# GDN and GLA heads on one Trainium2 core: a Sqrt of a constant ahead of the squares, and four pieces of work moved

## The chip, the cores and the metric

The program runs on one core of a Trainium2 chip. The time is device microseconds of one execution. Five engines work side by side and meet at semaphores: PE (matrix products), ACT (activations), DVE (vector work), POOL (vector work; here all its operands lie in SBUF), SP (here it only issues transfers). PE reads SBUF and writes PSUM.

## The reference

A four-layer trunk in one streaming step: 512 tokens of a new stream and 16 tokens of each of 8 running streams. Order of the parts: FFN, GLA mixer, FFN, FFN, gated-delta (GDN) mixer, FFN, each closed by a layer norm. The change lies in the two mixers. Of GDN, per value head and chunk:

```python
m = jnp.where(strict, jnp.einsum('bhid,bhjd->bhij', kb, kc) * decay, 0.0)
sol = lax.linalg.triangular_solve(eye + m, rhs, ...)     # w, u
v_new = u - jnp.einsum('bhid,bhdv->bhiv', w, s)
o = q_decayed @ s + att @ v_new
s = jnp.exp(g_last) * s + jnp.einsum('bhjd,bhjv->bhdv', k_end, v_new)
...
o = rms_norm(o, norm_g) * jax.nn.silu(z)                 # then @ w_o
```

q and k pass a short convolution, a silu and an l2 norm ahead of it. GLA has a recurrence of the same kind without the solve, and the same rms norm and silu gate.

## The kernel before

All 640 tokens stay in SBUF. Weights come in chunks of 128 columns, alternately into two buffers (`raw[0]`, `raw[1]`). ACT casts a chunk to `wh` (`act_split`, L246), POOL subtracts to get the rest `wl` (L283), and PE multiplies with both parts (L559 in the mixers, L228 in FFNs and projections). A chunk's buffer `wh` may be written again only when its tile of products is done.

Every engine runs its own program in the order in which it is written; nothing reorders. On PE the tile products of the *next* head are cut into 48 parts (`parts(a, b)`) that stand between the small products of the present head, so that PE has work while ACT and DVE prepare the next small product. GDN has 8 heads in two halves; after heads 3 and 7 stands an output projection. Head 7 has no next head: only parts 32 to 47 stand in it.

The steps of a GDN head that the change touches, in order:

- Start: PE transposes q and k (L544). ACT takes ten squares with a running sum (L1386), DVE adds epsilon (L1557), ACT takes the root (L1389), DVE inverts and scales (L1559, L1561, L1564, L1565). PE waits for that ahead of the transposes of v (L544 again).
- Later the four conv tiles of the next head come out of PSUM (`tile_out(0..3)`: three copies and a cast), and their silu (`conv_end`).
- Sequential part, t = 0 to 3: PE L1239, L1240, L1258, L1266, L1270; ACT `new_values` (L1443), `from_state` (L1437), `squares` (L1428); DVE `less_old` (L1665), the state (L1716), `outputs` (L1672). Then the running streams as a fifth step: PE L1275, L1281, L1292; DVE decays the eight streams' states in two halves (L1678), spreads values (L1684), adds outputs.
- Turn: DVE L1728, ACT root (L1461), DVE `new_stream(0)` (L1692), inverse (L1731), scaling of the outputs (L1734), `new_stream(1)`. PE transposes the outputs (L1300) when L1734 and both `new_stream` are done. ACT: silu of z (L1378) and cast of two tiles (`tile_out(4)`, `tile_out(5)`). DVE gates (L1698) and splits (L961, L963). PE goes on with the first part of the next head's conv tile (L559), which needs the `wl` of the chunk that `tile_out(4)` cast.

ACT holds one set of function tables at a time. A load (ACT_TABLE_LOAD) is put into ACT's program ahead of the first function that needs another set. Square and Copy need none of their own here; Sqrt, Exp and Silu do. In GLA the same pattern stands at a head's end: five squares (L849), DVE L937, root (L852).

Of the kernel before, what the change touches and what calls it, by code (L numbers as in the profile page):

```python
# [108 lines left out]
def build(nc, wstream, x_in, consts, ln_cols, w_a1, w_a2, b_a, norm_cols, w_ab, a_dt, conv_w, hist_in,  # L109
          gla_s, gdn_s, y_out, gla_p_out, gdn_p_out, hist_out, gla_s_out, gdn_s_out):  # L110
    with ExitStack() as ctx:
# [126 lines left out]
        def act_split(act, T, par):  # L238

            if isinstance(T, int) and T + 2 >= N_CHUNKS:  # L240
                return
            nxt = half(T) + 1
            act.wait_ge(loaded[par].sem, loaded[par].at(nxt))
            if not (isinstance(T, int) and T < 0):
                act.wait_ge(tile_done.sem, tile_done.at(T))
            act.copy(wh[:, par, :], raw[:, par, :]).then_inc(hi_ready.sem, hi_ready.by)  # L246
# [529 lines left out]
        def gla_loop(eng, body):  # L776
            with eng.Fori(0, GLA_HEADS - 1) as i:
                body(i)
            body(GLA_HEADS - 1, last=True)

        def act_gla(act, occ):
            b = base["gla", 0]

            def copy_in(T, par, j):
                act.wait_ge(tile_done.sem, tile_done.at(T))
                act.copy(halves(a_in[j]), slot(par)).then_inc(evacuated[par].sem, evacuated[par].by)
                act_split(act, T, par)
            copy_in(b, 0, 0)
            act.wait_ge(gla["rank_mm"].sem, gla["rank_mm"].at(0))
            act.copy(halves(a_rank), msc[:, 0:2, 0:HALF])\  # L790
               .then_inc(gla["rank"].sem, gla["rank"].by)
            copy_in(b + 1, 1, 1)
            for t in range(TT):
                ab = a_abs[:, t % 2, :]
                act.wait_ge(gla["logit_mm"].sem, gla["logit_mm"].at(0, t))
                if t >= 2:
                    act.wait_ge(gla["la"].sem, gla["la"].at(0, t - 2))
                act.activation(ab, msc[:, 2 + t % 2, :], ACT.Abs).then_inc(gla["logit_act"].sem, gla["logit_act"].by)
                act.wait_ge(gla["logit_act"].sem, gla["logit_act"].at(0, 3 * t))
                act.activation(ab, ab, ACT.Exp, scale=-1.0).then_inc(gla["logit_act"].sem, gla["logit_act"].by)  # L800
                act.wait_ge(gla["logit_act"].sem, gla["logit_act"].at(0, 3 * t + 1))
                act.activation(ab, ab, ACT.Ln, bias=ones[:, 0:1]).then_inc(gla["logit_act"].sem, gla["logit_act"].by)
            copy_in(b + 2, 0, 2)
            copy_in(b + 3, 1, 3)

            def body(i, last=False):
                h = i

                def tile_out(n):

                    j, par = GLA_ORDER[n], n % 2
                    if last and j < 4:
                        return
                    T = gla_tile(i, j)
                    act.wait_ge(tile_done.sem, tile_done.at(T))
                    if j >= 4:
                        act.activation(halves(a_z[j - 4]), slot(par), ACT.Silu).then_inc(evacuated[par].sem, evacuated[par].by)
                    else:

                        act.copy(halves(a_in[j]), slot(par)).then_inc(evacuated[par].sem, evacuated[par].by)  # L820
                    act_split(act, T, par)
                act.dma_start(a_sin.rearrange("p s d n -> p s (d n)"), gla_s[h]).then_inc(a_sld.sem, a_sld.by)
                act.wait_ge(gla["v_mm"].sem, gla["v_mm"].at(h, 0))
                act.copy(a_vt[:, :, 0:P], tiles5(pair[1])).then_inc(gla["v"].sem, gla["v"].by)
                act.wait_ge(gla["v_mm"].sem, gla["v_mm"].at(h, 1))
                act.copy(a_vt[:, :, P:2 * P], tiles5(pair[0])).then_inc(gla["v"].sem, gla["v"].by)
                act.wait_ge(gla["bs"].sem, gla["bs"].at(h))
                act.activation(a_e, a_bs, ACT.Exp, scale=1.0 / GATE_TAU).then_inc(gla["exp"].sem, gla["exp"].by)
                act.activation(a_en, a_bs, ACT.Exp, scale=-1.0 / GATE_TAU).then_inc(gla["exp"].sem, gla["exp"].by)
                act.wait_ge(gla["kdiff"].sem, gla["kdiff"].at(h))  # L830
                act.activation(a_kd, a_kd, ACT.Exp, scale=1.0 / GATE_TAU).then_inc(gla["kexp"].sem, gla["kexp"].by)
                tile_out(0)
                act.wait_ge(gla["ke_mm"].sem, gla["ke_mm"].at(h))
                act.copy(a_ket, tiles5(pair[0])).then_inc(gla["ke"].sem, gla["ke"].by)
                tile_out(1)
                for n in range(NCK):
                    if n % 2:
                        act.wait_ge(gla["o_mm"].sem, gla["o_mm"].at(h, n))
                        act.copy(a_o[:, n // 2, :], msc[:, (n // 2) % 2, 0:2 * P]).then_inc(gla["o"].sem, gla["o"].by)
                    if n in (2, 5):  # L840
                        tile_out(2 if n == 2 else 3)
                tile_out(4)
                act.wait_ge(gla["mid"].sem, gla["mid"].at(h))
                act.copy(a_o[:, PT, :], msc[:, 0, 0:2 * P]).then_inc(gla["o"].sem, gla["o"].by)
                for t in range(TT):
                    act.wait_ge(gla["o"].sem, gla["o"].at(h, t))
                    if t:
                        act.wait_ge(gla["sq"].sem, h * TT + t)
                    ins = act.activation(a_sq, a_o[:, t, :], ACT.Square, accum_out=a_ss[:, t:t + 1])  # L849
                    ins.then_inc(gla["sq"].sem, 1)  # L850
                act.wait_ge(gla["ss"].sem, gla["ss"].at(h))
                act.activation(a_std, a_ss, ACT.Sqrt).then_inc(gla["std"].sem, gla["std"].by)  # L852
                tile_out(5)

                act.wait_ge(gla["s_new"].sem, gla["s_new"].at(h, 1))
                act.dma_start(gla_s_out[h], a_sin.rearrange("p s d n -> p s (d n)")).then_inc(a_sst.sem, a_sst.by)
                act.dma_start(gla_p_out[h], a_s).then_inc(a_sst.sem, a_sst.by)
                act.wait_ge(a_sst.sem, a_sst.at(h, 1))
            gla_loop(act, body)
            act_projection(act, ("gla", 0), b + GLA_HEADS * 6, stats=True)  # L860

# [451 lines left out]
        def act_gdn(act, occ):  # L1313
# [46 lines left out]
            def body(hf, i, last=False):  # L1360
# [5 lines left out]
                        freed = (gdn["qk_mm"], s, j) if j < 2 else (gdn["v_mm"], s, j - 2)  # L1366
                        conv_out(j, s * 4 + (4 + j), freed)

                def tile_out(j):

                    T = gdn_tile(hf, i, j, last)
                    if j < 4:
                        if not last:
                            conv_in(T, j % 2, s * 4 + (4 + j), False)
                        return
                    act.wait_ge(tile_done.sem, tile_done.at(T))
                    act.wait_ge(gdn["att"].sem, gdn["att"].at(s, 1))
                    act.activation(halves(d_z[j - 4]), slot(j % 2), ACT.Silu).then_inc(evacuated[j % 2].sem, evacuated[j % 2].by)  # L1378
                    act_split(act, T, j % 2)
                for j in range(2):  # L1380
                    act.wait_ge(gdn["qk_mm"].sem, gdn["qk_mm"].at(s, j))
                    for t in range(TT):
# [35 lines left out]
                act.wait_ge(gdn["y_mm"].sem, gdn["y_mm"].at(s, product(LEVELS - 1, 1)))  # L1418
                act.dma_start(d_sin, gdn_s[s]).then_inc(d_sld.sem, d_sld.by)
                tile_out(3)  # L1420

                def squares(t):
                    for v in range(2):
# [21 lines left out]
                for t in range(PT):  # L1445
                    if t == 0:
                        new_values(t)
                        act.wait_ge(gdn["att"].sem, gdn["att"].at(s, 1))
                        from_state(t)
                    else:  # L1450
                        from_state(t)
                        new_values(t)
                        squares(t - 1)
                    if t == 3:
                        conv_end(3)
                from_state(PT)
                new_values(PT)
                squares(3)
                squares(4)
                act.wait_ge(gdn["oss"].sem, gdn["oss"].at(s))  # L1460
                act.activation(d_ors, d_os, ACT.Sqrt).then_inc(gdn["ostd"].sem, gdn["ostd"].by)  # L1461
                tile_out(4)
                tile_out(5)
                act.wait_ge(gdn["s_new"].sem, gdn["s_new"].at(s, 1))
                act.dma_start(gdn_s_out[s], d_sin).then_inc(d_sst.sem, d_sst.by)
                act.dma_start(gdn_p_out[s], d_s).then_inc(d_sst.sem, d_sst.by)
            for hf in range(2):
                gdn_in_line(hf, body)
                act_projection(act, ("gdn", 0), proj_start(hf), stats=hf == 1)

        def dve_gdn(dve, occ):
# [74 lines left out]
            def body(hf, i, last=False):  # L1546
# [154 lines left out]
                for t in range(PT):  # L1701
# [5 lines left out]
                        convolve(3, range(2 * t - 2, 2 * t))  # L1707
                    if t == 3:
                        less_old(PT)
                    dve.wait_ge(gdn["su_mm"].sem, gdn["su_mm"].at(s, t))  # L1710
                    if t == 0:
                        dve.wait_ge(gdn["s_zero"].sem, gdn["s_zero"].at(s))
# [6 lines left out]
                    ins.then_inc(gdn["state"].sem, gdn["state"].by)  # L1719
                    outputs(t)  # L1720
                key_ends(PT)
                decay_stream(0)
                decay_stream(1)
                dve.wait_ge(gdn["vn"].sem, gdn["vn"].at(s, PT))
                spread_values()
# [200 lines left out]
```

## Time and profile before

| | us |
|---|---|
| median of 3 runs (lowest, highest) | 3195.5 (3193.84, 3204.11) |
| profiled execution, own time | 3201.72 |
| its span, first to last instruction | 3199.8 |
| PE busy | 3043.3 (95%) |
| DVE, ACT, POOL busy | 1328.1, 1013.1, 994.8 |

GLA lies between about 505 and 840 us of the span, GDN between about 1830 and 2690. In a timeline row the first number is the start, the second the time taken, the bracket at its end the engine's idle time before it and what ended that. Busy time of PE does not tell at which clock it ran; the granted clock is a column of the stretches view.

### The profile page before, as it was taken

Reading aid. Unit: us, or ns where it says so; the run is one execution under the profiler, and the core shown is the slowest. Engines: PE = TensorE matmul, PEld = TensorE weight load, DVE = VectorE, ACT = ScalarE, POOL = GpSimd, SP = SyncE. Lnnn points to the kernel's source line nnn. Section 1 sums busy time; section 2 is a strip of 40 time slices with the busy share of each in tenths; the row PEclk is TensorE's granted clock in tenths of the full one; section 3 lists DMA queues with packets and bytes.
Section 4 is the critical chain, followed back from the end, with each engine's and each line's share of the span. In section 5 each row is a group of like instructions: output and inputs, shape, how many; then the busy total and the mean of one; then the engine's idle time right before and its main releaser. Section 6 shows DMA issues by size and latency. Waiting matters only on the chain.

```text
span 3199.8 us, 61556 instructions
## 1 busy us (share of the span) xinstructions
PE 3043.3 (95%) x25790; PEld 2904.8 (91%) x25790; DVE 1328.1 (42%) x1923; ACT 1013.1 (32%) x1751; POOL 994.8 (31%) x412
## 2 busy tenths in 40 slices
PE   8999999998999999999999989999999889999997
PEld 8999997887899999899999878888988778999997
DVE  3212253335521313621312666676376655312226
ACT  2111126333341111432111445444354434321112
POOL 3333343221433333433333411111211104333332
PEclk9999999999999999999999989999999979999998
DMA  3222221222122222122222111111111111222222
GB/s 132 73 77 80 74 82 51 81 75 83 60 73 74 79 79 77 64 74 77 73 86 73 63 45 62 62 69 63 67 62 69 63 43 53 79 73 79 80 73 78
DMA packets 62317, 230.60 MB, mean 72 GB/s; under 512 B 8257, under 2 KB 10177, under 8 KB 58754
## 3 DMA queue, kind: packets, MB, share of 16 engines
q1 hardware_dynamic: 56898, 200.27, 17.8%
q10 hardware_dynamic: 5184, 26.74, 2.2%
q8 instruction: 203, 3.33, 0.4%
q14 instruction: 32, 0.26, 0.0%
HBM read 209.76 MB, written 17.22 MB: 71 GB/s over the span
## 4 chain that ended last, share of the span: by engine, by line
PE 70%; issue 21%; POOL 4%; DVE 4%; ACT 1%; POOLq 0%; DVEq 0%; ACTq 0%
PE gem L228 60%; PE gem L559 4%; POOL wl L283 3%; POOL xl L509 1%; PE msc L420 1%; PE msc L435 1%; PE msc L726 1%; PE msc L734 1%; PE msc L544 0%; DVE work L497 0%; DVE work L925 0%; DVE work L928 0%; ACT small L1386 0%; PE msc L722 0%; DVE hh L961 0%
## 5 line engine op out<-in xcount | busy, mean ns | idle before, releaser
L283 POOL TENSOR_TENSOR wl<-raw,wh 128x1024 fp32r<-128x1024 f32 x368 | 931.9, 2533 | 2117.2 <-ACT wh L246 2117.2
L246 ACT CAST wh<-raw 128x1024 fp32r<-128x1024 f32 x368 | 386.5, 1050 | 1426.3 <-PE gem L228 1403.9
L228 PE MATMUL gem<-xh,wh 128*128 128x320 f32 x2688 | 612.6, 309 | 5.0 <-POOL wl L283 5.0
L228 PE MATMUL gem<-xl,wh 128*128 128x320 f32 x2688 | 612.5, 309 | 0.0
L228 PE MATMUL gem<-xh,wl 128*128 128x320 f32 x2688 | 612.4, 309 | 0.0
L228 PEld LDWEIGHTS gem<-xh,wh 128*128 128x128 f32 x2688 | 449.3, 188 | 5.9 <-ACT work L329 5.4
L228 PEld LDWEIGHTS gem<-xh,wl 128*128 128x128 f32 x2688 | 449.5, 188 | 0.0
L228 PEld LDWEIGHTS gem<-xl,wh 128*128 128x128 f32 x2688 | 449.3, 188 | 0.0
L350 DVE TENSOR_TENSOR work<-work,gem 128x640 f32<-128x640 f32 x88 | 72.3, 821 | 879.4 <-PE gem L228 843.4
L228 PE MATMUL gem<-hh,wh 128*128 128x320 f32 x1792 | 409.1, 310 | 2.1 <-issue 2.1
L228 PE MATMUL gem<-hl,wh 128*128 128x320 f32 x1792 | 408.9, 309 | 0.0
L228 PE MATMUL gem<-hh,wl 128*128 128x320 f32 x1792 | 408.8, 309 | 0.0
L559 PE MATMUL gem<-xh,wh 128*128 128x320 f32 x1184 | 302.6, 337 | 9.1 <-POOL wl L283 6.5
L228 PEld LDWEIGHTS gem<-hh,wh 128*128 128x128 f32 x1792 | 300.2, 188 | 2.5 <-issue 2.5
L228 PEld LDWEIGHTS gem<-hh,wl 128*128 128x128 f32 x1792 | 300.2, 188 | 0.0
L228 PEld LDWEIGHTS gem<-hl,wh 128*128 128x128 f32 x1792 | 300.0, 188 | 0.0
L378 DVE SCALAR_TENSOR_TENSOR x<-x,gem 128x640 f32 (+1 forms) x120 | 98.6, 822 | 482.1 <-PE gem L228 482.1
L559 PE MATMUL gem<-xl,wh 128*128 128x320 f32 x1184 | 274.4, 313 | 8.0 <-POOL xl L509 7.9
L559 PE MATMUL gem<-xh,wl 128*128 128x320 f32 x1184 | 272.3, 311 | 0.7 <-issue 0.6
L355 DVE TENSOR_TENSOR hl<-work,hh 128x640 f32 (+1 forms) x88 | 242.6, 2757 | 10.7
L559 PEld LDWEIGHTS gem<-xh,wh 128*128 128x128 f32 x1184 | 193.2, 192 | 35.9 <-issue 29.1
L559 PEld LDWEIGHTS gem<-xl,wh 128*128 128x128 f32 x1184 | 199.7, 190 | 13.2 <-POOL xl L509 13.2
(266 smaller groups left out, 2924.3 us busy)
## 6 DMA issues: line engine op xcount, KB each, us to landing
raw<-wstream SPq DMA_DIRECT2D x368, 512.0 KB, 3.5
work<-gdn_s ACTq DMA_DIRECT2D x8, 1024.0 KB, 5.0
gdn_s_out<-work ACTq DMA_DIRECT2D x8, 1024.0 KB, 4.0
work<-gla_s ACTq DMA_DIRECT2D x4, 1024.0 KB, 6.9
gla_s_out<-work ACTq DMA_DIRECT2D x4, 1024.0 KB, 4.0
x<-x_in SPq DMA_DIRECT2D x2, 1280.0 KB, 8.1
y_out<-x SPq DMA_DIRECT2D x8, 320.0 KB, 2.2
gdn_p_out<-work ACTq DMA_DIRECT2D x8, 128.0 KB, 4.0
```

What stands on the lines that cost most here:

```text
L228: mm = pe.matmul(gem[:, par, s, 0:HALF], w, r[:, k, s * HALF:(s + 1) * HALF], start=(k == 0 and n == 0), stop=(k == kts - 1 and n == 2))
L246: act.copy(wh[:, par, :], raw[:, par, :]).then_inc(hi_ready.sem, hi_ready.by)
L283: pool.tensor_tensor(wl[:, par, :], raw[:, par, :], wh[:, par, :].bitcast(F32), ALU.subtract)\
L350: dve.tensor_tensor(halves(hid), halves(gate), slot(1), ALU.mult)\
L355: dve.tensor_tensor(hl[:, i, :], hid, hh[:, i, :].bitcast(F32), ALU.subtract)\
L378: dve.scalar_tensor_tensor(out=halves(xt), in0=halves(xt), scalar=scale, in1=slot(par), op0=ALU.mult, op1=ALU.add).then_inc(evacuated[par] ...
L420: mm = pe.matmul(msc[:, 0, a * 8 + t:a * 8 + t + 1], src[:, t * P:(t + 1) * P], cs[:, C_MEAN:C_MEAN + 1], start=first and a == t == 0, sto ...
L435: pe.matmul(msc[:, b + s, 0:HALF], ones, flat[:, s * HALF:(s + 1) * HALF], start=True, stop=True)\
L509: pool.tensor_tensor(xl[:, k, :], x[:, k, :], xh[:, k, :].bitcast(F32), ALU.subtract)\
L559: mm = pe.matmul(gem[:, par, s, 0:HALF], w, r[:, k, s * HALF:(s + 1) * HALF], start=(k == 0 and n == 0), stop=(k == KT - 1 and n == 2))
L726: pe.matmul(msc[:, 2 + c, 0:2 * P], a_ket[rows, t, :], a_vt[rows, t, :], start=True, stop=True)\
L734: pe.matmul(msc[rows, t % 2, 0:2 * P], a_qd[:, n * GLA_CHUNK:(n + 1) * GLA_CHUNK], a_s, start=False, stop=True, skip_group_check=True)\
```

## The change

A new helper, `root_table`, takes the Sqrt of one constant column (128x1) into an unused column of `small`. It is called at three places: in GLA behind `tile_out(1)`, in a GDN head at its start, and in a GDN head behind `tile_out(3)`, ahead of the sequential part. The number of table loads in the program stays at 75. In the turn, the cast of `tile_out(4)` goes ahead of its silu; `conv_end(3)` goes from t = 3 to behind the two stores of the states; DVE's first half of the decay goes from behind the fifth step's `key_ends` to t = 3, ahead of the state update.

```diff
+        def root_table(act):
+            act.activation(small[:, 56:57], ones[:, 0:1], ACT.Sqrt)
...
                 tile_out(1)
+                root_table(act)
                 for n in range(NCK):
...
-                def tile_out(j):
+                def tile_out(j, split_done=False):
...
                     act.activation(halves(d_z[j - 4]), slot(j % 2), ACT.Silu).then_inc(...)
-                    act_split(act, T, j % 2)
+                    if not split_done:
+                        act_split(act, T, j % 2)
+                root_table(act)
                 for j in range(2):
                     act.wait_ge(gdn["qk_mm"].sem, gdn["qk_mm"].at(s, j))
...
                 tile_out(3)
+                root_table(act)
...
                         squares(t - 1)
-                    if t == 3:
-                        conv_end(3)
                 from_state(PT)
...
                 act.activation(d_ors, d_os, ACT.Sqrt).then_inc(gdn["ostd"].sem, gdn["ostd"].by)
-                tile_out(4)
+                act_split(act, gdn_tile(hf, i, 4, last), 0)
+                tile_out(4, split_done=True)
                 tile_out(5)
                 act.wait_ge(gdn["s_new"].sem, gdn["s_new"].at(s, 1))
                 act.dma_start(gdn_s_out[s], d_sin).then_inc(d_sst.sem, d_sst.by)
                 act.dma_start(gdn_p_out[s], d_s).then_inc(d_sst.sem, d_sst.by)
+                conv_end(3)
...
                     if t == 3:
                         less_old(PT)
+                        decay_stream(0)
...
                 key_ends(PT)
-                decay_stream(0)
                 decay_stream(1)
```

On ACT at the turn of a GDN head, from `conv_end(3)` (L1332) to the first cast (L246), before:

```order
L1332 ACTIVATE work<-work 128x512
L1333 ACTIVATE work<-work 128x128
L1437 ACTIVATE work<-msc,gq 128x128 x2
L1443 ACTIVATE work<-msc,gq 128x128 x2
L1428 ACTIVATE small,gq<-work 128x128 x4
L1461 ACT_TABLE_LOAD
L1461 ACTIVATE gq<-gq 128x10
L1378 ACT_TABLE_LOAD
L1378 ACTIVATE work<-gem 128x640
L246 CAST wh<-raw 128x1024
```

And of the changed kernel, from `new_values` of the fifth step (now L1451) to the load for the new Sqrt (L783) that opens the next head:

```order
L1451 ACTIVATE work<-msc,gq 128x128 x2
L1436 ACTIVATE small,gq<-work 128x128 x4
L1467 ACTIVATE gq<-gq 128x10
L246 CAST wh<-raw 128x1024
L1383 ACT_TABLE_LOAD
L1383 ACTIVATE work<-gem 128x640 x2
L246 CAST wh<-raw 128x1024
L1472 DMA gdn_s_out<-work 128x2048
L1473 DMA gdn_p_out<-work 128x256
L1337 ACTIVATE work<-work 128x512
L1338 ACTIVATE work<-work 128x128
L783 ACT_TABLE_LOAD
```

The load stands no longer between the last squares and the root, the first cast follows the root at once, and the silu of the conv tile stands behind the two stores.

On ACT ahead of the sequential part, from the load of the streams' states (DMA) on, before:

```order
L1419 DMA work<-gdn_s 128x2048
L1321 COPY work<-gem 128x320
L1322 COPY work<-gem 128x192
L1323 COPY work<-gem 128x8x16
L246 CAST wh<-raw 128x1024
L1443 ACTIVATE work<-msc,gq 128x128 x2
```

And of the changed kernel:

```order
L1426 DMA work<-gdn_s 128x2048
L1326 COPY work<-gem 128x320
L1327 COPY work<-gem 128x192
L1328 COPY work<-gem 128x8x16
L246 CAST wh<-raw 128x1024
L783 ACT_TABLE_LOAD
L783 ACTIVATE small<-cs 128x1
L1451 ACTIVATE work<-msc,gq 128x128 x2
```

A load and the new Sqrt stand between the cast of the fourth conv tile and `new_values` of t = 0.

On DVE at t = 3 and behind it (`less_old`, state, outputs, `key_ends`, decay, spread), before:

```order
L1665 SCALAR_TENSOR_TENSOR work<-msc,gq,work 128x128 x4
L1716 SCALAR_TENSOR_TENSOR work<-work,gq,msc 128x128 x2
L1672 TENSOR_TENSOR work<-work,msc 128x256
L1656 TENSOR_SCALAR work<-work,gq 128x128 x2
L1678 TENSOR_TENSOR work<-work,gq 128x1024 x2
L1684 TENSOR_SCALAR work<-work,cs 128x2x128 x2
```

And of the changed kernel:

```order
L1673 SCALAR_TENSOR_TENSOR work<-msc,gq,work 128x128 x4
L1686 TENSOR_TENSOR work<-work,gq 128x1024
L1725 SCALAR_TENSOR_TENSOR work<-work,gq,msc 128x128 x2
L1680 TENSOR_TENSOR work<-work,msc 128x256
L1664 TENSOR_SCALAR work<-work,gq 128x128 x2
L1686 TENSOR_TENSOR work<-work,gq 128x1024
L1692 TENSOR_SCALAR work<-work,cs 128x2x128 x2
```

One of the two decays now stands ahead of the state update. PE's, POOL's and SP's programs keep their order.

## Rows read from the trace of the kernel before

**Rows 1.** The chain that ended last, by engine, from the page

```profile
PE 70%; issue 21%; POOL 4%; DVE 4%; ACT 1%; POOLq 0%; DVEq 0%; ACTq 0%
```

**Rows 2.** Who PE waited for, GDN stretch: us in total, times, longest

```profile
PE msc L544 <- DVE work L1564: 8.3, 7, 6.3
...
PE msc L1275 <- ACT work L1437: 6.3, 7, 1.1
...
PE gem L559 <- POOL wl L283: 5.5, 5, 1.1
```

**Rows 3.** Timeline of PE, one turn (head 1 to head 2)

```profile
2043.68 0.71 PE L1275 MATMUL msc<-work 128*128 128x128 f32 x4 [0.85 <-ACT work L1437]
...
2047.59 1.15 PE L1292 MATMUL msc<-work 32*128 32x256 f32 x16 [0.89 <-DVE work L1672]
...
2052.94 1.28 PE L1300 MATMUL msc<-cs,work 128*128 128x128 f32 x10 [0.50 <-DVE work L1692]
...
2055.33 0.53 PE L559 MATMUL gem<-xh,wh 128*128 128x320 f32 x2 [1.11 <-POOL wl L283]
```

**Rows 4.** Timeline of ACT, the same turn and the squares behind it

```profile
2042.31 0.61 ACT L1332 ACTIVATE work<-work 128x512 f32<-128x512 f32 x1
...
2048.28 1.28 ACT L1461 ACT_TABLE_LOAD   x1
2049.57 0.21 ACT L1461 ACTIVATE gq<-gq 128x10 f32<-128x10 f32 x1
...
2051.70 1.04 ACT L246 CAST wh<-raw 128x1024 fp32r<-128x1024 f32 x1
...
2057.03 0.28 ACT L1386 ACTIVATE small<-msc 128x128 f32<-128x128 f32 x1 [2.75 <-PE msc L544]
...
2061.07 1.28 ACT L1389 ACT_TABLE_LOAD   x1
```

**Rows 5.** Timeline of DVE, the same turn

```profile
2042.87 0.61 DVE L1716 SCALAR_TENSOR_TENSOR work<-work,gq,msc 128x128 f32<-128x128 f32 x2 [2.16 <-PE msc L1270]
...
2044.11 2.36 DVE L1678 TENSOR_TENSOR work<-work,gq 128x1024 f32<-128x1024 f32 x2
...
2048.29 0.17 DVE L1728 TENSOR_SCALAR gq<-gq 128x10 f32<-128x10 f32 x1 [0.96 <-ACT small L1428]
2048.79 1.22 DVE L1692 TENSOR_TENSOR work<-work,msc 128x1024 f32<-128x1024 f32 x1 [0.33 <-PE msc L1292]
...
2050.17 1.49 DVE L1734 TENSOR_TENSOR work<-work,gq 128x1280 f32<-128x1280 f32 x1
```

**Rows 6.** Timeline of POOL, the same turn

```profile
2052.81 4.71 POOL L283 TENSOR_TENSOR wl<-raw,wh 128x1024 fp32r<-128x1024 f32 x2 [28.39 <-ACT wh L246]
```

**Rows 7.** Timeline of ACT at the start of a sequential part, head 2

```profile
2110.15 1.07 ACT L246 CAST wh<-raw 128x1024 fp32r<-128x1024 f32 x1
2111.74 0.62 ACT L1443 ACTIVATE work<-msc,gq 128x128 f32<-128x128 f32 x2 [0.52 <-PE msc L1258]
```

**Rows 8.** Timeline of DVE at the start of a sequential part, head 2

```profile
2110.86 0.82 DVE L1600 TENSOR_TENSOR work<-work 128x640 f32<-128x640 f32 x1
```

**Rows 9.** Timeline of DVE, the same place in head 1

```profile
2022.26 2.84 DVE L1600 TENSOR_TENSOR work<-work 128x640 f32<-128x640 f32 x1
```

**Rows 10.** Timeline of POOL, the same place in head 1

```profile
2022.04 2.38 POOL L283 TENSOR_TENSOR wl<-raw,wh 128x1024 fp32r<-128x1024 f32 x1 [20.07 <-ACT wh L246]
```

**Rows 11.** Busy time by stretch; behind POOL's: granted PE clock, DMA share, GB/s

```profile
2004.00:2021.00 17.00, 15.81 (x220) 13.96 (x206) 8.93 (x25) 5.40 (x18) 0.00 (x0) 0.61 0.14 44
...
2547.00:2551.00 4.00, 1.53 (x10) 1.06 (x10) 3.96 (x4) 2.79 (x16) 2.94 (x2) 0.93 0.91 328
2051.50:2056.50 5.00, 3.40 (x25) 2.95 (x24) 4.08 (x5) 2.78 (x4) 3.69 (x2) 1.00 0.56 225
```

**Rows 12.** Timeline of ACT at a GLA head's end

```profile
604.35 0.21 ACT L852 ACTIVATE small<-small 128x5 f32<-128x5 f32 x1 [3.03 <-DVE small L937]
```

**Rows 13.** Timeline of ACT behind `tile_out(1)` in the last GLA head

```profile
761.89 0.37 ACT L839 COPY work<-msc 128x256 f32<-128x256 f32 x1 [1.27 <-PE msc L734]
```

## The prediction

> **What bounds the kernel now.** I first read the chain that ended last: 70% of it is PE [rows 1]. An edit on ACT, DVE or POOL therefore counts only where PE waits for it. Then I read who PE waits for in the GDN stretch, and the timelines of PE, ACT, DVE and POOL round one turn. In 2040 to 2060 us PE stands still four times: 0.85 us ahead of L1275 (for ACT's `from_state`), 0.89 ahead of L1292 (for DVE's last `outputs`), 0.50 ahead of L1300 (for `new_stream(1)`), 1.11 ahead of the next head's L559 (for POOL's `wl`) [rows 3]. A fifth wait, ahead of the transposes of v, is for the scaling behind the first root: 8.3 us in 7 waits, 6.3 of it in one (head 7, which has no tile products to fill it), so 0.33 in each other [rows 2]. Together 3.7 us per turn. The reader is to see that these waits are links of one sequence: a gain in one moves the start of the next.
>
> **Part 1, fifth step.** `conv_end(3)` leaves the stretch between the squares of t = 2 and `from_state`. Its first silu begins at 2042.31 [rows 4], and PE waits 0.85 for what stands behind it [rows 3]; 6.3 us in 7 heads [rows 2]. `from_state` can start about 0.6 us earlier (0.61 and the tail of a shorter one; they overlap the next instruction). One decay goes to t = 3, where DVE stands idle for 2.16 us ahead of the state update [rows 5]. One decay is half of 2.36, or 1.18 us [rows 5], so that idle time covers it; were it gone, the state and all behind it would be up to 1.18 later. Behind the state only one decay is left, and spread and outputs follow 1.14 earlier (the other decay now ends about when the new values are there). L1292 starts 1.14 earlier: 0.6 of it from ACT, the rest out of the 0.89.
>
> **Part 2, the root of the turn.** The load of 1.28 us at 2048.28 goes [rows 4]. But DVE, between its L1728 and L1734, has `new_stream(0)` to do, which waits for L1292 and ends near 2050.0; the root with its load is done at 2049.78 [rows 4, 5]. So the load lay beside work, and removing it alone gives 0.
>
> **Part 3, the cast goes ahead.** In the old times: L1728 ends at 2048.46, the root of 0.21 at about 2048.7, the cast (1.04) at about 2049.7, and POOL starts some 0.07 behind a cast, as it does at 2052.81 behind the cast that ends at 2052.74 [rows 4 to 6]. So POOL starts near 2049.8 rather than at 2052.81, and the wait of 1.11 for `wl` goes. What is late next? POOL's instruction takes 2.36 (half of 4.71 [rows 6]), so it runs to about 2052.1, and L1734 becomes ready at 2050.17 [rows 5], inside it. In head 1, DVE's L1600, ready at 2022.26, met a POOL instruction of 2022.04 to 2024.42: it ended at 2025.10, 2.84 long, where the same line takes 0.82 in head 2 [rows 8 to 10]. It ended 0.68 behind POOL's end, so 0.14 of its 0.82 had been done in the wait. L1734, like L1600, reads two operands from SBUF and writes SBUF. If it waits in the same way, it ends 1.49 - 0.14 = 1.35 behind POOL's end: 2052.11 + 1.35 = 2053.46, in place of 2051.66, or 1.80 later. `new_stream(1)` and L1300 are 1.80 later with it. Bounds of this term: 0, if L1734 gets in ahead of POOL or doesn't mind it, and 2.0, if the small inverse ahead of L1734 waits too. I take 1.80: POOL is ready about 0.4 us ahead of L1734, more than the error of these sums.
>
> On this the Trainium skill (GPSIMD Engine Reference, 8. Key points) says that GpSimd shares its SBUF interfaces with VectorE and contends with DVE instructions in a 2-port perf mode or with two SBUF inputs. By that rule L1734 is one that collides, and L1692 and L1698, which read PSUM, are not; the trace agrees as far as L1600 goes, and shows no L1734 under a POOL instruction.
>
> So L1300 starts 1.80 - 1.14 = 0.66 later than before, at 2053.6, and PE waits there 2.3 us, not 0.50. It ends at about 2054.9, `wl` is long there, and L559 starts 0.4 earlier than at 2055.33.
>
> **Part 4, the next head's start.** ACT now issues two stores and then does the silu of `conv_end(3)` (0.9), a load (1.28) and the new Sqrt (0.2) ahead of the squares. ACT stood idle for 2.75 us there [rows 4]; with the stores waiting for the later `new_stream(1)` it is ready about when the transposes are, some 0.3 earlier than at 2057.03. Behind the squares the load at 2061.07 is gone [rows 4]; the root still waits for L1557, so 1.05 to 1.1 us is left as gain, and the wait of 0.33 ahead of the transposes of v goes. Turn in all: 0.40 + 0.33, or 0.73 earlier.
>
> **Part 5, ahead of the sequential part.** Here the new load is on the path. The cast ends at 2111.22 and `new_values` starts at 2111.74, as soon as PE's L1258 lets it [rows 7]. With 1.28 and 0.21 in between it starts near 2112.7: 0.93 later. PE does one part meanwhile and is at L1266 when the new values come; the rest of the step goes through them. So 0.93 in each of heads 0 to 6. Head 7 has no fourth tile there and pays 0. Bounds: 0.5 to 1.0.
>
> The Trainium skill (ScalarE: Activation LUTs, What ACT_TABLE_LOAD costs) gives about 1283 ns for the load and 1380 more for a drain. The load is confirmed; the Sqrt behind the load starts at 2049.57, 0.01 after it, so no drain of that length is seen. By the page this part would cost 2.3 us a head, an estimate.
>
> **Part 6, GLA.** The root there waits for DVE (3.03 idle [rows 12]) and the load lies in that; removing it gives 0. Its new place has 1.27 idle in the tightest head [rows 13], against 1.49: 0.2 late in a copy that PE needs over 1 us later. 0 in all.
>
> **The sum.** Turns 0-1, 1-2, 2-3, 4-5 and 5-6: 5 x 0.73 = 3.7 gained. Turns into the two projections: 0.4 and 0.3 gained (no gain behind them: head 4's squares now start behind ACT's load, which takes what the missing one gives). Turn 6-7: 0.15 lost (L1300 later, no tile product to regain it). Together 4.2 gained. Heads 0 to 6: 7 x 0.93 = 6.5 lost. Net 2.3 us slower. The profiled execution would go from 3201.72 to 3204.0. It stands 6.2 above the median; head 1 in it lost about 17 x 0.39 = 6.6 us to the clock at 0.61 in one 17 us stretch [rows 11], which need not fall in every run. From the median of 3195.5 I forecast 3198.
>
> **Rivals.** First, L1734 gets in ahead of POOL, or they don't collide there. Then L1300 starts 1.14 earlier, the `wl` wait of 1.11 goes as well, and behind the squares 0.2 more (there ACT's own silu and load are the bound): 2.45 a turn, 5 x 2.45 + 2.25 + 2.25 + 0.9 = 17.7, less 6.5: 3184. For it: only 0.4 us of lead. Against it: POOL's start hangs on one short root and one cast of known length, L1734 on PE's L1292 and 1.22 of DVE. 17%.
>
> Second, slower: the longer waits bring the granted clock to its lower level. Over 2547 to 2551 us, where PE was busy 1.53 of 4.00 with transposes alone, the clock fell to 0.93 of that stretch and on; in 2051.5 to 2056.5, busy 3.40 of 5.00, it stayed at 1.00 [rows 11]. By the main case the turn holds 2.3 us of rest and 1.28 of transposes in one piece. The price of one fall, from the stretch in head 1, is up to 6.6 us: one gives 3204, two 3211. It decides from two falls on. 18%.
>
> Third, a load holds ACT for longer than its own row, say twice its 1.28 [rows 4], at the place where PE waits for it. Seven times 1.28 is 9.0 more: 3207. The drain of the Trainium skill's page above would be such a hold. The root that starts 0.01 behind its load [rows 4] speaks against it. 3%.
>
> That nothing changes at all (the loads keep their number, 75) falls into the main case's range.
>
> **How the numbers follow.** Main case 62%, its own range 3192 to 3203. Rival one 17%, two 18%, three 3%. The range is to hold the time 8 times in 10: 3185 to 3208, cutting off half of the first rival and the worse part of the second. A measurement of this kernel tells 0.3%, or 9.6 us, from no change (its three runs lie 10 us apart). Faster by that is the first rival alone, and not quite all of it: 0.16. Slower: two falls or more, or the drain, 0.18. The rest, 0.66, is no change.
>
> **What would show it.** In the changed profile: L1275's wait down to about 0.2 and L1292's to about 0.4; decay at t = 3 inside DVE's idle time; the L1734 line (then L1742) near 3.2 us long, not 1.49, under POOL's instruction; PE's wait ahead of L1300 (then L1305) near 2.3; none for `wl` behind it; a new wait of about 0.9 ahead of L1266 (then L1271) in seven heads. The forecast is wrong if L1742 is 1.49 long (then it is faster), or if PE doesn't wait at L1271.

## The result, and the profile after

Over 20 runs each the changed kernel takes 3205.76 us in the median (3199.74 to 3213.59), the kernel before 3196.73 (3192.27 to 3205.71). The ratio is 1.0024, 95% interval 1.0017 to 1.0031: 7.7 us slower (5.4 to 9.9), below the 0.3% that the prediction set as a bound, and inside its range. Forecast were 2.3 us more. The profiled execution takes 3201.40 us, 4 below its median; that of before stood 5 above its own.

What PE waits for in the GDN stretch (answers to [rows 2]; total, times, longest):

```profile
PE msc L1305 <- DVE work L1700: 18.5, 8, 2.4
...
PE msc L544 <- DVE work L1572: 5.6, 2, 5.3
PE msc L1271 <- ACT work L1451: 5.0, 7, 0.7
...
PE msc L1297 <- DVE work L1680: 3.7, 8, 0.5
...
PE msc L544 <- ACT work L1400: 2.6, 6, 0.5
```

The wait for `wl` (5.5) is gone, `from_state` and `outputs` (6.3 and 7.5) have shrunk to about 1.1 and 3.7. In their place: 18.5 ahead of the turn's transposes (L1305, before 4.0) and 5.0 ahead of L1271, which PE waited for once before.

The turn from head 1 to head 2, on PE (answers to [rows 3]):

```profile
2035.38 0.71 PE L1280 MATMUL msc<-work 128*128 128x128 f32 x4
...
2038.86 1.15 PE L1297 MATMUL msc<-work 32*128 32x256 f32 x16 [0.46 <-DVE work L1680]
...
2046.13 1.93 PE L1305 MATMUL msc<-cs,work 128*128 128x128 f32 x10 [2.41 <-DVE work L1700]
```

The same on ACT (to [rows 4]), DVE (to [rows 5]) and POOL (to [rows 6]):

```profile
2039.87 0.21 ACT L1467 ACTIVATE gq<-gq 128x10 f32<-128x10 f32 x1 [0.24 <-DVE gq L1736]
2039.99 1.03 ACT L246 CAST wh<-raw 128x1024 fp32r<-128x1024 f32 x1
```

```profile
2033.03 1.21 DVE L1686 TENSOR_TENSOR work<-work,gq 128x1024 f32<-128x1024 f32 x1
2035.28 0.61 DVE L1725 SCALAR_TENSOR_TENSOR work<-work,gq,msc 128x128 f32<-128x128 f32 x2 [1.03 <-PE msc L1275]
...
2041.44 3.41 DVE L1742 TENSOR_TENSOR work<-work,gq 128x1280 f32<-128x1280 f32 x1
```

```profile
2041.10 2.40 POOL L283 TENSOR_TENSOR wl<-raw,wh 128x1024 fp32r<-128x1024 f32 x1 [22.89 <-ACT wh L246]
```

This is the main case of the prediction: POOL starts 0.34 us ahead of the scaling, the scaling takes 3.41 us and not 1.49, and PE rests 2.41. The first decay lies inside idle time of DVE.

The start of a sequential part, on ACT (answers to [rows 7]) and PE:

```profile
2014.47 1.07 ACT L246 CAST wh<-raw 128x1024 fp32r<-128x1024 f32 x1
2015.56 1.28 ACT L783 ACT_TABLE_LOAD   x1
2016.85 0.20 ACT L783 ACTIVATE small<-cs 128x1 f32<-128x1 f32 x1
2016.96 0.61 ACT L1451 ACTIVATE work<-msc,gq 128x128 f32<-128x128 f32 x2
```

```profile
2015.34 0.69 PE L1263 MATMUL msc<-work 128*128 128x128 f32 x4
2017.62 0.71 PE L1271 MATMUL msc<-work 128*128 128x128 f32 x4 [0.72 <-ACT work L1451]
```

The same two products on PE before, head 2:

```profile
2111.02 0.69 PE L1258 MATMUL msc<-work 128*128 128x128 f32 x4
...
2112.43 0.70 PE L1266 MATMUL msc<-work 128*128 128x128 f32 x4
```

From start to start it was 1.41 us and is 2.28, so the new load costs 0.87 a head, 6.1 in seven heads. The bracket says only 0.72: it counts from the end of the product before, and without a wait L1266 starts 0.16 ahead of that end.

What was not in the main case stands in the stretches view: two turns, 0-1 and 1-2 (us, busy time of PE, PEld, DVE, ACT, POOL; behind POOL's the granted clock; answers to the last line of [rows 11]).

```profile
1956.80:1962.60 5.80, 3.50 (x30) 3.22 (x29) 4.84 (x6) 3.82 (x6) 2.39 (x2) 1.00 0.72 271
2043.40:2050.40 7.00, 4.59 (x26) 4.32 (x25) 5.74 (x7) 3.96 (x6) 2.46 (x2) 0.76 0.74 259
```

Both have nearly the same rest (2.30 and 2.41). In the second the clock fell to its lower level: the ten transposes take 1.93 us there and 1.28 in the first (next rows, PE, then ACT's first square), and the squares start 4.35 behind them and not 3.20. Up to the squares, one fall costs the turn 1.15 us.

```profile
1959.44 1.28 PE L1305 MATMUL msc<-cs,work 128*128 128x128 f32 x10 [2.30 <-DVE work L1700]
```

```profile
1962.64 0.26 ACT L1393 ACTIVATE small<-msc 128x128 f32<-128x128 f32 x1
...
2050.48 0.28 ACT L1393 ACTIVATE small<-msc 128x128 f32<-128x128 f32 x1 [1.08 <-PE msc L544]
```

Further on it is more. The turn from L1275 of t = 3 to the first L1151 of the next head, turn 0-1 and then 1-2:

```profile
1948.04 0.61 PE L1275 MATMUL msc<-work 128*128 128x128 f32 x4
...
1974.27 2.39 PE L1151 MATMUL msc<-work 128*128 128x128 f32 x20
```

```profile
2034.63 0.61 PE L1275 MATMUL msc<-work 128*128 128x128 f32 x4
...
2062.54 2.39 PE L1151 MATMUL msc<-work 128*128 128x128 f32 x20
```

And turn 1-2 before:

```profile
2042.22 0.61 PE L1270 MATMUL msc<-work 128*128 128x128 f32 x4
...
2069.10 2.39 PE L1146 MATMUL msc<-work 128*128 128x128 f32 x20
```

That is 26.23 us without a fall, 27.91 with one, and 26.88 before. So a fall costs 1.6 to 1.7 (turn 2-3 takes 27.83), and a turn without one is 0.65 shorter than before.

Four of the eight turns of this execution fall at the wait; before, all eight stayed up. What decides it isn't shown: the shortest rest (2.24, turn 2-3) is among those that fall, and three turns with 2.30 don't. That the two profiled executions are equally long comes from another fall: that of before has the loss of up to 6.6 us in head 1 [rows 11], this one has not.

### The profile page after: what moved, and what is told of

Same layout as the page of the kernel before. It is cut to its first block, busy times and chain, and to the rows that moved or that the text cites. A ratio compares the mean times of both kernels' runs of the same rounds, so it can differ in the third digit from the quotient of the medians.

```text
span 3199.5 us, 61576 instructions
## 1 busy us (share of the span) xinstructions
PE 3043.8 (95%) x25790; PEld 2908.1 (91%) x25790; DVE 1324.2 (41%) x1923; ACT 1017.6 (32%) x1771; POOL 995.8 (31%) x412
## 4 chain that ended last, share of the span: by engine, by line
PE 81%; DVE 8%; issue 5%; ACT 3%; POOL 2%; DVEq 0%; ACTq 0%; POOLq 0%
PE gem L228 62%; PE gem L559 9%; POOL xl L509 2%; PE msc L420 1%; DVE work L1500 1%; PE msc L435 1%; PE msc L544 1%; PE msc L1184 1%; DVE work L1597 1%; PE msc L1176 1%; PE msc L726 1%; PE msc L734 1%; PE msc L1271 1%; POOL wl L283 1%; PE msc L1151 0%
## 5 line engine op out<-in xcount | busy, mean ns | idle before, releaser
L246 ACT CAST wh<-raw 128x1024 fp32r<-128x1024 f32 x368 | 386.3, 1050 | 1425.1 <-PE gem L228 1403.6
L559 PE MATMUL gem<-xh,wh 128*128 128x320 f32 x1184 | 301.8, 336 | 4.0 <-issue 1.6
L559 PE MATMUL gem<-xl,wh 128*128 128x320 f32 x1184 | 274.0, 313 | 6.6 <-POOL xl L509 6.5
L559 PE MATMUL gem<-xh,wl 128*128 128x320 f32 x1184 | 272.0, 311 | 0.4 <-issue 0.3
L559 PEld LDWEIGHTS gem<-xh,wh 128*128 128x128 f32 x1184 | 192.9, 191 | 28.8 <-issue 22.1
L559 PEld LDWEIGHTS gem<-xl,wh 128*128 128x128 f32 x1184 | 199.4, 190 | 11.0 <-POOL xl L509 10.8
```

Of the source, the lines that this page charges most:

```text
L559: mm = pe.matmul(gem[:, par, s, 0:HALF], w, r[:, k, s * HALF:(s + 1) * HALF], start=(k == 0 and n == 0), stop=(k == KT - 1 and n == 2))
```

## The experiments

The theory after this reading: the excess is the collision at the turn, plus the falls in the rest that it makes, plus the seven waits ahead of L1271 (5.0 us by their brackets). Each kernel was timed against the kernel before on the same chip; differences are the ratio less one, times 3196.

| kernel | against before, us (95%) |
|---|---|
| changed kernel | +7.7 (5.4 to 9.9) |
| e1: no Sqrt ahead of the sequential part | -18.9 (-24 to -13) |
| e2: cast behind its silu | -11.8 (-17 to -7) |
| e3: neither | -11.8 (-17 to -7) |
| e4: 16 products in the rest | +9.6 (5.4 to 14) |
| e5: that Sqrt in idle time | +1.9 (-1.3 to 4.8) |
| e6: scaling ahead of `new_stream(0)` | -10.9 (-15 to -6.7) |
| e7: e5 and e6 | -18.5 (-22 to -15) |
| e8: 9 products in the rest | +2.9 (0.0 to 5.8) |
| e9: decay alone | -9.9 (-14 to -6.1) |
| e10: silu alone | -2.2 (-5.8 to 1.0) |
| e11: e7 without the Sqrt at the head's start | -16.9 (-21 to -13) |

**e1, e2, e3: the two suspects, crossed.** From the changed kernel:

```diff
 # e1 and e3
                 tile_out(3)
-                root_table(act)
 # e2 and e3
-                act_split(act, gdn_tile(hf, i, 4, last), 0)
-                tile_out(4, split_done=True)
+                tile_out(4)
```

> The changed kernel without the new Sqrt behind tile_out(3); all else stays. The load of 1.28 us then comes back between the last squares and the root of the turn. Theory (two parts): the wait of 0.72 us ahead of L1271 goes in heads 0 to 6, so 5.0 us less; and the cast of the turn ends 1.28 later, so POOL's instruction is ready near 2042.4 in the times of the changed trace, behind the start of the DVE scaling (2041.44). The scaling then takes 1.49 us and not 3.41, PE's wait ahead of its transposes shrinks from 2.3 to about 0.4 or less, and no turn falls to the lower clock. Together 12 to 18 us faster than the kernel before. Rival: the early Sqrt costs its 5.0 us and nothing else hangs on it (POOL still gets in first, or the load at the turn is itself waited for): 2 to 4 us slower than before, scaling still 3.4 long.

> The changed kernel with the cast of tile 4 put back behind its silu; the early Sqrt stays. Theory: POOL starts near 2043.3 (changed trace's times), the scaling takes 1.49 us, the wait of 2.3 ahead of the turn's transposes is about 0.4, no turn falls to the lower clock, and a wait for wl of about 0.2 to 0.7 comes back at L559; the 0.72 in seven heads stays. 8 to 13 us faster than before. Rival (the turn's collision costs little, since PE would wait for wl in its place, and the excess lies in the early Sqrt alone): wl wait back at about 1.1 or more, 0 to 4 us slower than before.

> The changed kernel without the Sqrt behind tile_out(3) and with the cast of tile 4 behind its silu: what is left is the decay at t = 3, conv_end(3) behind the stores, the Sqrt at a head's start and the one in GLA. Theory: 0.6 to 1.14 us per turn from the fifth step and 0.33 behind the squares, wl wait still near 1.1, no wait at L1271: 7 to 11 us faster than before, less than the version with the cast ahead and no early Sqrt by about 5 to 7. Rival (what the fifth step gains is lost again in the wl wait, which is bound by the casts): within 3 us of before.

All three went as the theory said in the main. e1 (18.9 faster) and e3 (11.8) lie a little past their ranges, and in e2 the wait for `wl` that was expected back did not come. In e1 the load stands at the turn again. ACT, DVE and POOL there, turn 5-6:

```profile
2440.16 1.28 ACT L1466 ACT_TABLE_LOAD   x1
2441.46 0.21 ACT L1466 ACTIVATE gq<-gq 128x10 f32<-128x10 f32 x1
2441.57 1.03 ACT L246 CAST wh<-raw 128x1024 fp32r<-128x1024 f32 x1
```

```profile
2442.06 1.49 DVE L1741 TENSOR_TENSOR work<-work,gq 128x1280 f32<-128x1280 f32 x1
```

```profile
2442.69 3.12 POOL L283 TENSOR_TENSOR wl<-raw,wh 128x1024 fp32r<-128x1024 f32 x1 [22.97 <-ACT wh L246]
```

The load holds the cast back by its 1.28, so the scaling comes first, and now POOL waits (3.12 and not 2.40). In e2 the early Sqrt keeps its price, the scaling is free; in e3 the wait for `wl` is back:

```profile
PE msc L1271 <- ACT work L1451: 5.1, 7, 0.7
...
PE msc L1305 <- DVE work L1699: 4.0, 8, 0.5
```

```profile
PE gem L559 <- POOL wl L283: 5.5, 5, 1.1
```

In e2, L559 follows the transposes at once:

```profile
2442.83 1.28 PE L1305 MATMUL msc<-cs,work 128*128 128x128 f32 x10 [0.50 <-DVE work L1699]
2444.16 0.53 PE L559 MATMUL gem<-xh,wh 128*128 128x320 f32 x2
```

So e2 and e3 take the same time, but the early Sqrt is not free: it costs 0.87 a head ahead of L1271, and as it takes the load from ahead of the turn's cast, it saves the wait for `wl`. Neither edit is bad by itself: the cast ahead is worth 7 us without the early Sqrt (e1 against e3; the intervals overlap, but a turn takes 24.5 us in the one trace and 25.7 in the other) and costs 19.5 with it.

**e6: the collision by DVE's order alone.** From the changed kernel, cast and Sqrt untouched:

```diff
-                new_stream(0)
                 dve.wait_ge(gdn["ostd"].sem, gdn["ostd"].at(s))
...
+                new_stream(0)
                 new_stream(1)
```

> The changed kernel with one step of DVE moved: the scaling of the outputs (inverse and L1742) goes ahead of new_stream(0). Cast and both Sqrt stay where they are. Theory (POOL's instruction, once begun, keeps out a DVE instruction with two SBUF operands, and the other way round): the scaling starts near 2040.5 in the changed trace's times, ahead of POOL (2041.1); it takes 1.49 us, POOL's first instruction about 3.0, both new_stream about 1.2 each although POOL runs beside them; PE's wait ahead of the transposes is about 0.5, no turn falls to the lower clock. The 0.72 in seven heads stays. 9 to 14 us faster than before. Rival (new_stream is held in the scaling's place, 3.1 to 3.4 long): wait of 2.3 stays, 5 to 9 us slower than before.

As the theory said. DVE and POOL, turn 5-6:

```profile
2446.27 1.49 DVE L1741 TENSOR_TENSOR work<-work,gq 128x1280 f32<-128x1280 f32 x1
2447.68 2.35 DVE L1700 TENSOR_TENSOR work<-work,msc 128x1024 f32<-128x1024 f32 x2
```

```profile
2447.01 3.03 POOL L283 TENSOR_TENSOR wl<-raw,wh 128x1024 fp32r<-128x1024 f32 x1 [22.78 <-ACT wh L246]
```

Both `new_stream` run beside POOL at full speed (2.35 for two); one operand of theirs lies in PSUM.

**e5 and e7: the price ahead of the sequential part.**

```diff
                 tile_out(3)
-                root_table(act)
...
                     if t == 0:
...
                         from_state(t)
+                        root_table(act)
```

> The changed kernel with the Sqrt that stands behind tile_out(3) put behind from_state of t = 0, where ACT stands idle for 2.57 us (changed trace). Cast, scaling and the wait of 2.3 at the turn stay. Theory: only the seven waits of 0.72 ahead of L1271 go, 5.0 us; so 2 to 4 us slower than before, L1742 still 3.4 long. Rival (the step at t = 0 has room behind it and the 0.72 is given back there): 7 to 8 us slower than before, like the changed kernel.

> Both of the two edits of this call together: the Sqrt ahead of the sequential part behind from_state of t = 0, and DVE's scaling ahead of new_stream(0). Theory: neither the 0.72 nor the 2.3 is left, 15 to 20 us faster than before, about the same as the kernel without the early Sqrt (18.3 faster). Rival (either price is not what it seems): 9 to 14 us faster or less.

e5 is 5.8 us below the changed kernel, where the seven delays were 6.1; L1305 still waits 18.4 in its trace. e7 has neither wait and is as fast as e1 (their intervals overlap almost wholly): PE waits ahead of its L1305 are

```profile
PE msc L1305 <- DVE work L1700: 3.6, 8, 0.5
```

**e4 and e8: the falls, with the rest kept.** Extra products that nobody reads, ahead of the wait (e4 the like with 16, in five turns):

```diff
                 parts(44, 48)
+                pe.wait_ge(evacuated[0].sem, evacuated[0].at(half(gdn_tile(hf, i, 4, last))))
+                for k in range(9):
+                    pe.matmul(gem[:, 0, 0, HALF:HALF + P], d_kq[:, 0, col(k % 4)], d_kq[:, 1, col(k % 4)], ...)
                 pe.wait_ge(gdn["on"].sem, gdn["on"].at(s))
```

> The changed kernel with 16 extra products of 128x128 on PE (0.12 us each, 1.95 in all) into unused columns of PSUM, in the wait ahead of the turn's transposes, in heads 0, 1, 2, 4 and 5. They change no result and end before the wait does. Theory (falls of the clock): PE no longer rests 2.3 us, the granted clock stays at its upper level in these five turns, and the 1.15 us that a fall cost in the changed trace (squares 4.35 behind the transposes, not 3.20) go: 3 to 6 us less than the changed kernel, so 2 to 5 slower than before. Rival (the falls cost nothing in the end, or come at other places): same as the changed kernel, 7 to 8 us slower than before.

> The changed kernel with 9 extra products on PE in the wait ahead of the turn's transposes, in all eight heads; the 16 of the run before took 3.57 us a turn in its trace, not the 1.95 that was reckoned, and so ran past the wait. 9 take 2.0 of the 2.3 us. Theory (falls of the clock cost 1.15 us each, in about five of eight turns of an ordinary run): the clock stays up in the turns, 1 to 4 us slower than before. Rival (the falls cost nothing in the end): 7 to 8 us slower than before, like the changed kernel.

e4 missed: its products take 3.6 us a turn (one call is two passes of about 0.11), which I had read off a row of 20 passes as 20 calls.

```profile
L1304 PE MATMUL gem<-work 128*128 128x128 f32 x31 | 3.6, 275 | 0.0
```

They ran past the wait (no idle time ahead of its transposes), so the time of e4 says nothing on what the falls cost. With 9, the transposes wait 0.3 and start when they would have; the clock stays up in every turn (two of them):

```profile
1958.00:1964.00 6.00, 5.70 (x49) 5.50 (x48) 5.04 (x6) 3.75 (x5) 2.61 (x2) 1.00 0.67 255
2045.50:2051.40 5.90, 5.51 (x48) 5.31 (x47) 4.94 (x6) 3.81 (x6) 2.58 (x2) 1.00 0.69 261
```

e8 is 4.8 us below the changed kernel. The same four turns, from L1275 to L1151, are 5.5 us shorter in its trace. So work that computes nothing made the kernel faster. The two intervals overlap by 0.3 us, so the size is rough; that the turns no longer fall is shown.

**e9 and e10: which move serves the fifth step.** Kernel before, with only `decay_stream(0)` at t = 3 (e9), or only `conv_end(3)` behind the stores (e10):

> The kernel before with DVE's first decay at t = 3 and nothing else. Theory: the wait ahead of L1292 shrinks from 0.89 to about 0.3 to 0.5, the 0.85 ahead of L1275 stays since ACT's silu still stands there; 0.4 to 0.6 a turn, 3 to 5 us faster than before in all. Rival (the late from_state sets the outputs of the fifth step anyway): within 1 us of before.

> The kernel before with conv_end(3) behind the two stores and nothing else. Theory: the wait ahead of L1275 shrinks from 0.85 to 0.14, but DVE's two decays (2.36 us) then set the outputs of the fifth step, and the wait ahead of L1292 grows by about as much, to 1.4 to 1.6; within 1.5 us of before, so that the two moves are worth much only together. Rival (the two gains add up): 4 to 5 us faster than before by itself.

The waits of e9, then of e10:

```profile
PE msc L1275 <- ACT work L1437: 6.3, 7, 1.1
...
PE msc L1292 <- DVE work L1672: 0.5, 1, 0.5
```

```profile
PE msc L1292 <- DVE work L1671: 12.5, 8, 1.6
...
PE msc L1275 <- ACT work L1437: 0.4, 1, 0.4
```

e10 is as expected: what leaves the wait for ACT goes into that for DVE. e9 missed: the decay removes the whole 0.89, not half of it, in eight heads 7.0 of the 9.9 us (start to start 0.96 a head). Behind the late `from_state` there was room for one decay, but not for two.

**e11: the Sqrt at a head's start.** e7 without it:

> The fastest version so far (Sqrt behind from_state of t = 0, scaling ahead of new_stream(0)) without the Sqrt at the start of a GDN head, so that its load of 1.28 stands behind the squares again. Theory: the squares start about 0.7 us earlier, the root comes about 0.6 later, and PE waits that much more ahead of the transposes of v; 0.3 to 0.6 a head, 2 to 4 us slower than that version, so 14 to 18 faster than before. Rival (PE's first parts hide it): no difference, 18 to 20 faster than before.

The times leave it open: 1.6 us slower than e7, with intervals that overlap widely. PE's waits ahead of the transposes of e11 name DVE again:

```profile
PE msc L544 <- DVE work L1571: 8.5, 7, 6.3
```

In e7 the same line waits 6.3 for DVE and 1.8 for ACT (L1400), 8.1 in all. So the move changes for whom PE waits, and hardly how long. The traces bear out the rival: from L1275 of t = 3 to the first L1151, turn 2-3 takes 24.38 us in both.

## Why the prediction was right, and where a term was off

**Part 1** holds in sum: L1275's 0.85 became 0.14, L1292's 0.89 became 0.46, which is the 1.14 forecast. Its split ("0.6 of it from ACT, the rest out of the 0.89") is wrong: e9 gives 0.96 by the decay alone (L1292 starts 1.52 behind L1281, before 2.48), e10 nothing by the silu alone, and together they give 0.18 more.

**Part 2** is wrong in "removing it alone gives 0". The root's result was not late, but the cast stands behind the root, and `wl` behind the cast. e2 and e3 differ by the early Sqrt alone: with the load at the turn PE waits 1.10 for `wl`, without it not at all. The sum was spared, since Part 3 counts that wait as gone by the cast.

**Part 3** holds: the scaling takes 3.41 (forecast 3.2), the rest is 2.3 to 2.4 (2.3), `wl` is never waited for, POOL's lead is 0.34 (0.4). The Trainium skill (GPSIMD Engine Reference, 8. Key points) names two SBUF inputs, or a 2-port perf mode, as what contends; here the scaling is held and `new_stream`, with one input in PSUM, is not, as e6 shows. The first rival would have needed 0.34 us: e1 and e6 are that rival made true, in two ways. Its price was right: 2.45 a turn and 11.2 in all were forecast, e6 has 2.5 (24.4 us a turn against 26.9) and 10.9.

**Part 4** gave nothing where 0.33 stood. The wait ahead of the transposes of v went, but one of 0.3 to 0.5 came ahead of the next transposes, for ACT's copy L1400 (2.6 us in 6 waits). That copy stands behind `tile_out(0)`, which waits for PE's own tile product. In its place L559 of an unfallen turn came 0.67 earlier, where Part 3 has 0.40: in turn 0-1 it starts 12.44 behind L1275, before 13.11. The two errors cancel, which was luck: 0.65 a turn in all, forecast 0.73.

**Part 5** holds: 0.87 in each of seven heads, 6.1 us, where 0.93 and 6.5 stood. `new_values` starts 1.42 us behind the cast; a drain of 1380 ns on top of the load, as the Trainium skill has it (ScalarE: Activation LUTs, What ACT_TABLE_LOAD costs), is not there: the Sqrt starts 0.01 us after the load.

**Part 6** holds: GLA's root now shows 4.33 us of idle time ahead of it, which is the 3.03 of [rows 12] and the load:

```profile
603.38 0.21 ACT L857 ACTIVATE small<-small 128x5 f32<-128x5 f32 x1 [4.33 <-DVE small L942]
```

**The sum.** Turns without a fall and the new load came out within 0.1 us each of what was forecast, and the main case's +2.3 stands close to e8, where the rest is filled: +2.9. What lacks to 7.7 is the second rival, which was not instead of the main case but on top of it. Its mechanism was right and its price was not: a fall costs 1.6 to 1.7 us in turns 1-2 and 2-3, not 6.6, since it ends with the turn (the clock is at 1.00 again over 2050 to 2055), and the trace has four. How many other executions have is not known. I had priced it from a stretch of 17 us of small products, and left it out of the likeliest case at 18%. So that the time lies in the range is owed to the width of the range, not to the 2.3.

## What to carry to other kernels

A transfer of work to an earlier time is worth what it uncovers: ask which instruction of another engine will then start beside it, and whether both have their operands in SBUF. Here 0.34 us of lead decided over 19.5 us, and a slower step ahead of the cast, or another order on DVE, won them back. Two moves that serve one wait are priced together: here the decay alone gave 0.96 us a head, the silu alone nothing. What a wait costs is read from start to start in two traces: the bracket of a wait alone gave 0.72 for 0.87. A forced rest of PE costs more than its length where the clock falls in it, and that price is read from the turns of one trace that fall and those that don't.

## What the runs showed of the hardware

The exclusion goes both ways: POOL's instruction, ready 0.63 to 0.74 us behind the scaling's start, takes 3.12 and 3.03 us and not 2.40, and ends 2.26 to 2.28 behind the scaling. And a DVE cast with a single SBUF operand is held too: in e1 L966, alone 0.48, under POOL's second instruction.

```profile
2447.20 1.77 DVE L966 CAST hh<-work 128x640 fp32r<-128x640 f32 x1
```

```profile
2446.24 2.38 POOL L283 TENSOR_TENSOR wl<-raw,wh 128x1024 fp32r<-128x1024 f32 x1 [0.43 <-ACT wh L246]
```
